# TensorE's expert program as a loop over pairs of experts, with every weight chunk in a fixed slot of the ring

## The chip, the cores and the metric

One core of one Trainium2 chip. The metric is the device time of one launch in microseconds (us): 1264.06 us, the median of 3 runs (1262.40 to 1265.34). One more execution was taken by the hardware profiler; it took 1263.88 us, of which 1262.1 us are the span of the trace, and 1.8 us lie outside it.

## The reference

One decoder block on 256 tokens of width 1024, float32. Two groups of four heads with gated recurrences share an input and an output projection; cross-attention into 256 memory tokens follows; then a mixture of 32 experts of which each token uses 4; then a norm. The experts are what matters here:

```
logits = h2 @ w_router + b_router ; top_v, top_i = top_k(logits, 4) ; gates = softmax(top_v)
for every expert e, on the tokens that chose it:
    gu = x @ w_gate_up[e] + b_gate_up[e]          # w_gate_up[e]: 1024 x 2048
    gate, up = min(gu[:, :1024], 7), clip(gu[:, 1024:], -7, 7)
    y += g * (((up + 1) * gate * sigmoid(1.702 * gate)) @ w_down[e] + b_down[e])   # w_down[e]: 1024 x 1024
```

The weights of one expert are 12.6 MB in float32, those of all 32 are 403 MB, and every one of them is read.

## The kernel before

The program is written out by hand for five engines, which meet only at semaphores. For the first 335 us TensorE does projections, recurrence, attention and router; then it does the experts one after the other.

An expert's weights come as six chunks of 2 MB (128 partitions x 4096 float32): chunks 0 to 3 are gate and up, 4 and 5 are down. Below, chunk e.k is chunk k of expert e, and its number is 6e+k. The chunks go through a ring of 11 places (`places`, `RING`), of which six double as the earlier panels' buffers and five as working buffers of the earlier stages. Chunk n has place n modulo 11. Chunks 0 to 10 are loaded by SyncE (SP) as their places come free in the earlier stages. From then on SP runs the loop

```
for n in range(RING, LOADS):
    before, k = (n - RING) // CHUNKS, (n - RING) % CHUNKS
    ...
    sp.wait_ge(sem["chunk_used"], sp.snap(used + (k + 1)))
    load_chunk(n)
```

so that chunk n is asked for once chunk n-11 has been used. SP works strictly in order: one load that waits holds all that come behind it. `chunk_used` is raised by TensorE after the last matmul on a chunk. How many chunks TensorE will have used by the end of an expert depends on the routing (an expert with more than 64 tokens is run again on the next 64), so SP reads that number from a table in memory. In this run every expert takes one block of 64.

TensorE's work for one expert (`pe.Fori(0, blocks)`): biases; 16 matmuls for each of chunks 0 to 3 (`pair`, L730, on the columns 0-63 and 64-127 of the array); `scatter` of the expert before (L740); a transpose of gates (L797); `gather` of the next expert's tokens (48 bf16 matmuls, L754, which pick the input features f of a tile with a stride through `h2_parts`); four transposes of the activations (L805); then 16 matmuls for each of chunks 4 and 5. All 32 experts are written out, each with its own places and its own counts as constants. VectorE and ScalarE follow in loops of their own.

Of the kernel before, what the change touches and what calls it, by code (L numbers as in the profile page):

```python
# [41 lines left out]
P = 128  # L42
D = 1024
T = 256
NT = T // P
KT = D // P
# [10 lines left out]
E = 32  # L57
# [3 lines left out]
ROWS = 64  # L61
MAXB = T // ROWS
# [3 lines left out]
GU_ROWS = KT // GU_CHUNKS  # L66
DOWN_ROWS = KT // DOWN_CHUNKS
LOADS = CHUNKS * E
RING = 11
MAXW = MAXB * E  # L70
WARM_UP = 14
BIAS_PARTS = (0, 2 * E, 3 * E)
PW = 512
# [39 lines left out]
def build(nc, A, out):  # L113

    ctx = ExitStack()
    with ctx:
        ctx.enter_context(nc.allow_non_contiguous_dma("small vectors are laid out by feature"))

        def sb(name, cols, dt=F32, rows=P):
            return ctx.enter_context(nc.sbuf_tensor(name, [rows, cols], dt))  # L120
# [12 lines left out]
        ring = sb("ring", SLOTS * 4096)  # L133
        slot6, slot7, slot8, slot9, slot10 = (sb(f"slot{k}", 4096) for k in range(6, 11))
        region5, region6 = slot6[:, 0:2048], slot6[:, 2048:4096]
        region1, region2 = slot7[:, 0:2048], slot7[:, 2048:4096]
        x_res_t, region10 = slot8[:, 0:2048], slot8[:, 2048:4096]
        s_t, row_t = slot9[:, 0:3072], slot9[:, 3072:4096]
        region3, tmp_t, late = slot10[:, 0:2048], slot10[:, 2048:3072], slot10[:, 3072:4096]
# [14 lines left out]
        def tm(t, off=0, n=D):  # L154

            return t[:, off:off + NT * n].rearrange("p (t n) -> p t n", n=n)
# [88 lines left out]
        def panel(n):  # L245

            s = n % SLOTS
            return ring[:, s * 4096:(s + 1) * 4096].rearrange("p (k n) -> p k n", n=PW)
# [3 lines left out]
        out_tile = tm(slot9, 0)  # L252
# [28 lines left out]
        def _(sp):  # L281
# [22 lines left out]
            def load_chunk(n):  # L304

                e, k = n // CHUNKS, n % CHUNKS
                dst, arrived = places[n % RING], chunk_in[n % RING]
# [5 lines left out]
                rows = DOWN_ROWS * P  # L313
                src = A["w_down"][0, e, (k - GU_CHUNKS) * rows:(k - GU_CHUNKS + 1) * rows, :].rearrange("(p a) n -> p (a n)", a=DOWN_ROWS)
                if n < LOADS - 1:
                    sp.dma_start(dst, src).then_inc(arrived, 16)
                    return
                half = DOWN_ROWS * D // 2
                sp.dma_start(dst[:, 0:half], src[:, 0:half]).then_inc(arrived, 16)
                sp.dma_start(dst[:, half:2 * half], src[:, half:2 * half]).then_inc(last_half_in, 16)  # L320

            wait_full(sp, "out11")
            load_chunk(0)
            wait_full(sp, "xq1")
            load_chunk(1)
            wait_full(sp, "xq3")
            load_chunk(2)
            wait_full(sp, "xv11")
            load_chunk(3)

            wait_full(sp, "pv3")
            load_chunk(4)
            load_chunk(5)
            wait_full(sp, "xo01")
            load_chunk(6)
            wait_full(sp, "xo11")
            load_chunk(7)

            load_chunk(8)
# [3 lines left out]
            load_chunk(9)  # L343
# [4 lines left out]
            load_chunk(10)  # L348
# [95 lines left out]
        def _(pe):  # L444
# [300 lines left out]
            def gather(ready):  # L745

                pe.wait_ge(sem["sel_ready"], ready)
                for c in range(GU_CHUNKS):
                    for a in range(GU_ROWS):
                        k = c * GU_ROWS + a  # L750
                        first = c * GU_ROWS * P + a
                        for i in range(3):
                            for t in range(NT):
                                last = pe.matmul(bank_a[:, k * ROWS:(k + 1) * ROWS],  # L754
                                                 h2_parts[:, i, t, first:first + GU_ROWS * P - a:GU_ROWS], sel[:, t, :],
                                                 start=(i == 0 and t == 0), stop=(i == 2 and t == NT - 1), skip_group_check=True)
                last.then_inc(sem["xb_psum"], 1)

            def chunk_of(e, k):

                n = e * CHUNKS + k
                return places[n % RING], chunk_in[n % RING], 16 * (n // RING + 1)
# [6 lines left out]
            for e in range(E):  # L769
                blocks = pe.value_load(table[0:1, e:e + 1], min_val=1, max_val=MAXB)  # L770
                first = pe.value_load(table[0:1, e + E:e + E + 1], min_val=0, max_val=MAXW)
                with pe.Fori(0, blocks) as c:
# [7 lines left out]
                    for k in range(GU_CHUNKS):  # L780
                        wk, arrived_k, count = chunk_of(e, k)
                        pe.wait_ge(arrived_k, count)
                        for a in range(GU_ROWS):
                            f = k * GU_ROWS + a
# [19 lines left out]
                    for a in range(DOWN_ROWS):  # L804
                        last = pe.matmul(bank_u[:, a * P:(a + 1) * P], act_t[:, a::DOWN_ROWS], ident[:, :], start=True,  # L805
                                         stop=True, is_transpose=True, skip_group_check=True)
# [4 lines left out]
                    for j in range(DOWN_CHUNKS):  # L811
                        wk, arrived_k, count = chunk_of(e, GU_CHUNKS + j)
                        pe.wait_ge(arrived_k, count)
                        for a in range(DOWN_ROWS):
                            if e == E - 1 and j == DOWN_CHUNKS - 1 and a == DOWN_ROWS // 2:
                                pe.wait_ge(last_half_in, 16)
                            f = DOWN_ROWS * j + a
                            last = pair(bank_d, actT[:, f, :], wk[:, a * D:(a + 1) * D], f == 0, f == KT - 1)
                        last.then_inc(sem["chunk_used"], 1)

# [619 lines left out]
```

## Time and profile before

| | |
|---|---|
| time, median of 3 runs | 1264.06 us |
| profiled execution / its span | 1263.88 us / 1262.1 us |
| TensorE matmuls busy (PE) | 1162.4 us, 92% |
| VectorE, ScalarE, GpSimd busy | 21%, 14%, 2% |
| read from HBM | 443.4 MB |
| loads of expert chunks | 46.4 to 47.9 us from issue to landing (medians) |
| the chain that ended last | PE 58%, DMA 38% |

PE's busy time is modelled at the ends of the matmuls, and in the experts' stage two matmuls run side by side in the array, so 92% does not say that TensorE is the bound. SPq is the queue of DMA issues that SP works through. "To landing" is the time from a DMA's issue to the last of its completions.

### The profile page before, as it was taken

The numbers are of one execution on the slowest core, as the hardware profiler recorded it, in microseconds if no ns is written. First come the engines' busy times: TensorE is split into PE (matmuls) and PEld (weight loads), VectorE is DVE, ScalarE is ACT, GpSimd is POOL, SyncE is SP. The second block draws the span as 40 slices with busy tenths as digits, with TensorE's granted clock in tenths as the row PEclk, the third lists the DMA queues.
The fourth block names the chain that finished last, engine by engine and source line by source line (L and its number), as shares of the span: only waits on it lengthen the run. The fifth ranks groups of instructions, "written<-read, shape, count | busy, mean of one in ns | idle before, by whom it ended". The sixth has DMA issues, their size and how long they took to land.

```text
span 1262.1 us, 16197 instructions
## 1 busy us (share of the span) xinstructions
PE 1162.4 (92%) x6670; PEld 567.8 (45%) x6670; DVE 268.7 (21%) x626; ACT 173.3 (14%) x284; POOL 28.0 (2%) x60
## 2 busy tenths in 40 slices
PE   8999999999799999999998888888888888888885
PEld 5955875875544444444443333333333333333332
DVE  4334455113612111121111111111111111111112
ACT  3222111023301110011100000010110010000001
POOL 3000010010200000000000000000000000000000
PEclk9999999999899999999999999999999999999999
DMA  8933300576799999999999999999999999999993
GB/s 262 365 133 133 133 10 1 210 257 241 274 419 426 429 427 427 428 427 428 426 428 427 428 428 426 428 427 427 428 428 427 427 427 427 427 429 427 427 427 138
DMA packets 53055, 445.42 MB, mean 353 GB/s; under 512 B 8896, under 2 KB 9312, under 8 KB 28192
## 3 DMA queue, kind: packets, MB, share of 16 engines
q1 hardware_dynamic: 52560, 442.87, 84.6%
q0 software_dynamic: 432, 1.59, 0.5%
q8 instruction: 54, 0.88, 0.3%
q14 instruction: 9, 0.07, 0.0%
HBM read 443.40 MB, written 1.05 MB: 352 GB/s over the span
## 4 chain that ended last, share of the span: by engine, by line
PE 58%; DMA 38%; issue 2%; DVE 2%; ACT 0%; SPq 0%; DVEq 0%
PE bank L730 26%; DMA ring<-in_w_gate_up 19%; DMA slot<-in_w_gate_up 19%; PE bank L504 12%; PE bank L495 7%; PE bank L740 3%; PE bank L754 3%; PE bank L515 2%; PE bank L474 1%; PE bank L805 1%; DMA ring<-in_w_in 1%; PE bank L797 1%; PE bank L617 1%; PE bank L668 1%; PE bank L649 1%
## 5 line engine op out<-in xcount | busy, mean ns | idle before, releaser
L730 PE MATMUL bank<-ring,region 128*64 128x512 f32 x1696 | 381.0, 596 | 41.7 <-DMA ring<-in_w_gate_up 28.3
L730 PE MATMUL bank<-slot,region 128*64 128x512 f32 x1376 | 309.9, 595 | 36.0 <-DMA slot<-in_w_gate_up 25.6
L730 PEld LDWEIGHTS bank<-ring,region 128*64 128x64 f32 x1696 | 133.7, 137 | 264.2 <-issue 207.2
L730 PEld LDWEIGHTS bank<-slot,region 128*64 128x64 f32 x1376 | 107.6, 137 | 218.2 <-issue 165.7
L1360 DVE TENSOR_SCALAR region<-bank 128x512 f32<-128x512 f32 x32 | 22.1, 691 | 713.3 <-PE bank L730 713.3
L504 PE MATMUL bank<-ring,slot 128*128 128x512 f32 x352 | 153.5, 594 | 0.1
L829 ACT ACTIVATE region<-bank 128x512 f32<-128x512 f32 (+2 forms) x136 | 72.8, 544 | 344.4 <-PE bank L730 231.2
L504 PEld LDWEIGHTS bank<-ring,slot 128*128 128x128 f32 x352 | 66.3, 190 | 79.9 <-issue 78.9
L829 ACT ACTIVATE bank<-region 128x512 f32<-128x512 f32 x32 | 19.3, 602 | 498.7 <-DVE region L1360 498.7
L495 PE MATMUL bank<-slot,ring 128*128 128x256 f32 x384 | 84.2, 380 | 0.0
L495 PEld LDWEIGHTS bank<-slot,ring 128*128 128x128 f32 x384 | 72.6, 190 | 10.4 <-issue 0.5
L740 PE MATMUL bank<-region 64*128 64x512 f32 x264 | 65.6, 615 | 0.7 <-ACT region L829 0.7
L754 PE MATMUL bank<-region,r_levels 128*128 128x64 bf16 x1584 | 52.8, 195 | 1.6 <-DVE region L1341 1.6
L754 PEld LDWEIGHTS bank<-region,r_levels 128*128 128x128 bf16 x1584 | 51.7, 99 | 2.2 <-issue 1.6
L740 PEld LDWEIGHTS bank<-region 64*128 64x128 f32 x264 | 22.7, 186 | 43.1 <-issue 41.5
L829 ACT ACTIVATE slot<-bank 128x512 f32<-128x512 f32 (+1 forms) x35 | 19.9, 586 | 100.7 <-PE bank L504 61.0
L1341 DVE TENSOR_SCALAR region<-region 128x64 bf16 (+1 forms) x64 | 13.3, 251 | 48.6 <-PE bank L754 45.8
L515 PEld LDWEIGHTS bank<-r_levels 128*128 128x128 f32 (+1 forms) x240 | 21.9, 189 | 3.6 <-issue 2.4
L1363 DVE TENSOR_SCALAR region<-bank 128x512 f32<-128x512 f32 x32 | 22.1, 691 | 5.3 <-PE bank L730 5.3
L805 PE MATMUL bank<-ident,region 128*128 128x128 f32 x128 | 23.2, 304 | 0.0
L515 PE MATMUL bank<-r_levels 128*128 128x128 f32 (+1 forms) x240 | 23.0, 281 | 0.0
L1367 DVE SCALAR_TENSOR_TENSOR region<-region 128x512 f32<-128x512 f32 x32 | 22.2, 692 | 3.3
(181 smaller groups left out, 493.8 us busy)
## 6 DMA issues: line engine op xcount, KB each, us to landing
ring<-in_w_gate_up SPq DMA_DIRECT2D x70, 2048.0 KB, 46.4
slot<-in_w_gate_up SPq DMA_DIRECT2D x58, 2048.0 KB, 47.9
ring<-in_w_down SPq DMA_DIRECT2D x36, 2048.0 KB, 47.8
slot<-in_w_down SPq DMA_DIRECT2D x27, 2048.0 KB, 47.6
ring<-in_w_in SPq DMA_DIRECT2D x7, 2048.0 KB, 19.4
ring<-in_w_xkv SPq DMA_DIRECT2D x4, 2048.0 KB, 8.0
ring<-in_w_out SPq DMA_DIRECT2D x2, 2048.0 KB, 7.6
ring<-in_w_xq SPq DMA_DIRECT2D x2, 2048.0 KB, 7.8
```

The costliest lines, as they stand in the source:

```text
L495: last = pe.matmul(bk[:, i * T:(i + 1) * T], w[:, k, (m + i) * P:(m + i + 1) * P], rhs[:, k, :], start=(k == 0), stop=(k == KT - 1))
L504: last = pe.matmul(bk[:, :], lhs[:, k, t * P:(t + 1) * P], w[:, k, :], start=(k == 0), stop=(k == KT - 1))
L515: return pe.matmul(out_, rows[:, j * P:(j + 1) * P], rows[:, i * P:(i + 1) * P], start=True, stop=True)
L730: last = pe.matmul(bk[half * ROWS:(half + 1) * ROWS, :], lhs, w[:, half * 512:(half + 1) * 512], start=start, stop=stop, skip_group_check= ...
L740: last = pe.matmul(bank_y[t][half][:, :], combT[rows, t * P:(t + 1) * P], yb[rows, :], start=False, stop=False, skip_group_check=True)
L754: last = pe.matmul(bank_a[:, k * ROWS:(k + 1) * ROWS], h2_parts[:, i, t, first:first + GU_ROWS * P - a:GU_ROWS], sel[:, t, :], start=(i == ...
L805: last = pe.matmul(bank_u[:, a * P:(a + 1) * P], act_t[:, a::DOWN_ROWS], ident[:, :], start=True, stop=True, is_transpose=True, skip_group ...
L829: return nc.scalar.activation(out_, in_, func, **kw)
L1341: ins = v.tensor_scalar(sel[:, t, :], rows, rank_m[:, t, e], None, ALU.is_equal)
L1360: v.tensor_scalar(g_t, bank_g[:, :], LIMIT, None, ALU.min).then_inc(sem["g_clamped"], 1)
L1363: v.tensor_scalar(u_t, bank_u[:, :], LIMIT, -LIMIT, ALU.min, ALU.max).then_inc(sem["u_clamped"], 1)
L1367: v.scalar_tensor_tensor(u_t, u_t, 1.0, g_t, ALU.add, ALU.mult).then_inc(sem["up_gated"], 1)
```

## The change

TensorE's 32 copies of an expert become 4 written-out experts (0 to 3, `HALVED`), a loop `pe.Fori(0, PAIRS)` of 13 passes with two experts in its body (4 to 29), and 2 written-out experts (30 and 31). A loop body needs the same addresses in every pass, so a chunk's place can no longer be n modulo 11. The new `slot_of` keeps the old places up to chunk 11 and then repeats every 12 chunks; a wait's count becomes a register that grows with the pass. The 11 slots are now one tensor, with the earlier buffers laid in so that chunks 0 to 10 lie over the same buffers as before.

```diff
-GU_ROWS = KT // GU_CHUNKS
+ROWS_PER = 4
+GU_TILES = KT // GU_CHUNKS
 RING = 11
+HALVED = 4
+PAIRS = (E - HALVED) // 2 - 1
...
-        places = [ring[:, s * 4096:(s + 1) * 4096] for s in (5, 1, 2, 0)] + [slot6[:, :], slot9[:, :]]
-        places += [ring[:, s * 4096:(s + 1) * 4096] for s in (3, 4)] + [slot7[:, :], slot8[:, :], slot10[:, :]]
+        def slot_of(e, k):
+
+            n = e * CHUNKS + k
+            if n <= RING:
+                return n % RING
+            if (e, k) == (E - 1, CHUNKS - 2):
+                return 0
+            j = n % (2 * CHUNKS)
+            return j + 1 if j < RING - 1 else j - 5
+
+        order = [(e, k) for e in range(E) for k in range(CHUNKS)]
+        loads_of = [[c for c in order if slot_of(*c) == s] for s in range(RING)]
+
+        def nth_load(e, k):
+            return loads_of[slot_of(e, k)].index((e, k)) + 1
+
+        def used_before(e, k):
+
+            return loads_of[slot_of(e, k)][nth_load(e, k) - 2]
...
-            def load_chunk(n):
+            def load_chunk(e, k):
...
-                    rows = GU_ROWS * P
-                    src = A["w_gate_up"][0, e, k * rows:(k + 1) * rows, :].rearrange("(p a) n -> p (a n)", a=GU_ROWS)
+                    rows, c0 = ROWS_PER * P, k % 2 * SLOT
+                    src = A["w_gate_up"][0, e, k // 2 * rows:(k // 2 + 1) * rows, :].rearrange("(p a) n -> p (a n)", a=ROWS_PER)
+                    sp.dma_start(dst, src[:, c0:c0 + SLOT]).then_inc(arrived, 16)
...
-            for n in range(RING, LOADS):
-                before, k = (n - RING) // CHUNKS, (n - RING) % CHUNKS
-                if k == 0 or n == RING:
-                    used = sp.value_load(table[0:1, before + 2 * E + 1:before + 2 * E + 2], min_val=0, max_val=CHUNKS * MAXW)
-                sp.wait_ge(sem["chunk_used"], sp.snap(used + (k + 1)))
-                load_chunk(n)
+            for e, k in order[RING:]:
+                before, kb = used_before(e, k)
+                used = sp.value_load(table[0:1, before + 2 * E + 1:before + 2 * E + 2], min_val=0, max_val=CHUNKS * MAXW)
+                sp.wait_ge(sem["chunk_used"], sp.snap(used + (kb + 1)))
+                load_chunk(e, k)
...
-                                                 h2_parts[:, i, t, first:first + GU_ROWS * P - a:GU_ROWS], sel[:, t, :],
+                                             h2_parts[:, i, t, c + a:c + ROWS_PER * P:ROWS_PER], sel[:, t, :],
...
-            for e in range(E):
+            for e in range(HALVED):
+                expert(e, slots(e), counts(e))
+            with pe.Fori(0, PAIRS) as i:
+                for odd in range(2):
+                    e = HALVED + odd
+                    per_pair = [n1 - n0 for n0, n1 in zip(counts(e), counts(e + 2))]
+                    n = {(m, n0): pe.snap(m * i + n0) for m, n0 in sorted(set(zip(per_pair, counts(e))))}
+                    expert(pe.snap(2 * i + e), slots(e), [n[m, n0] for m, n0 in zip(per_pair, counts(e))])
+            for e in range(E - 2, E):
+                expert(e, slots(e), counts(e), e == E - 1)
```

A gate-and-up chunk also holds other rows: before, partition p of chunk k had rows 2p and 2p+1 of 256 consecutive rows, so the chunk was 2 MB in one piece of memory. Now chunks 0 and 1 share 512 rows: partition p has rows 4p and 4p+1 of them in chunk 0 and 4p+2 and 4p+3 in chunk 1. A partition's piece is 16 KB as before, and the next partition's begins 32 KB on. The gather's stride through `h2_parts` goes from 2 to 4 elements with it.

TensorE's program shows the slots. First the two down chunks of expert 2, the biases of expert 3, and its chunks, in the program before (`chunk_in5` is the arrival semaphore of place 5; 64x512 is what one matmul writes):

```order
L730 MATMUL bank<-slot,region 64x512 [waits chunk_in5,actT_ready,comb_ready]
...
L730 MATMUL bank<-ring,region 64x512 [waits chunk_in6]
...
L730 MATMUL bank<-region 64x512 [waits one_hot_ready]
...
L730 MATMUL bank<-ring,region 64x512 [waits chunk_in7,xb_ready]
...
L730 MATMUL bank<-slot,region 64x512 [waits chunk_in8]
...
L730 MATMUL bank<-slot,region 64x512 [waits chunk_in9]
...
L730 MATMUL bank<-slot,region 64x512 [waits chunk_in10]
...
L730 MATMUL bank<-ring,region 64x512 [waits chunk_in0,actT_ready,comb_ready]
...
L730 MATMUL bank<-ring,region 64x512 [waits chunk_in1]
```

And the same place in the program after:

```order
L753 MATMUL bank<-ring,region 64x512 [waits chunk_in5,actT_ready,comb_ready]
...
L753 MATMUL bank<-ring,region 64x512 [waits chunk_in6]
...
L753 MATMUL bank<-region 64x512 [waits one_hot_ready]
...
L753 MATMUL bank<-ring,region 64x512 [waits chunk_in7,xb_ready]
...
L753 MATMUL bank<-ring,region 64x512 [waits chunk_in8]
...
L753 MATMUL bank<-ring,region 64x512 [waits chunk_in9]
...
L753 MATMUL bank<-ring,region 64x512 [waits chunk_in10]
...
L753 MATMUL bank<-ring,region 64x512 [waits chunk_in5,actT_ready,comb_ready]
...
L753 MATMUL bank<-ring,region 64x512 [waits chunk_in6]
```

Chunks 3.4 and 3.5 stood in slots 0 and 1; they now stand in slots 5 and 6, where chunks 2.4 and 2.5 are. Slot 0 is not used again until chunk 31.4. From expert 2 on the slots repeat: 1, 2, 3, 4, 5, 6 for an even expert and 7, 8, 9, 10, 5, 6 for an odd one.

SP's program is still written out, one load after the other. Before, from the load of chunk 20 to that of chunk 23:

```order
L311 DMA slot<-in_w_gate_up 128x4096 [waits chunk_used]
L354 REGISTER_ALU
L311 DMA slot<-in_w_gate_up 128x4096 [waits chunk_used]
L354 REGISTER_ALU
L316 DMA ring<-in_w_down 128x4096 [waits chunk_used]
L353 TENSOR_LOAD region
L353 ISA x2
L354 REGISTER_ALU
L316 DMA ring<-in_w_down 128x4096 [waits chunk_used]
```

After, from the load of chunk 20 to that of chunk 22:

```order
L335 DMA ring<-in_w_gate_up 128x4096 [waits chunk_used]
L376 TENSOR_LOAD region
L376 ISA x2
L377 REGISTER_ALU
L335 DMA ring<-in_w_gate_up 128x4096 [waits chunk_used]
L376 TENSOR_LOAD region
L376 ISA x2
L377 REGISTER_ALU
L340 DMA ring<-in_w_down 128x4096 [waits chunk_used]
```

The table is now read ahead of every load (L376), before only when the wait passed to another expert's chunks (L353). What the rows don't name is the count that is waited for: chunk 22 (3.4) waited for chunk 11 (1.5) and now waits for chunk 16 (2.4), chunk 23 for chunk 17 in place of 12, chunk 24 for chunk 12 in place of 13. From there on chunks 4 and 5 of an expert wait for chunks 4 and 5 of the expert before (6 back), and chunks 0 to 3 for those of two experts before (12 back).

The loop's end in TensorE's program after (L789 is the loop over blocks, L846 the loop over pairs):

```order
L753 MATMUL bank<-ring,region 64x512 [waits chunk_in6]
L753 MATMUL bank<-ring,region 64x512 x7
L789 REGISTER_ALU
L789 COMPARE_AND_BRANCH
L846 REGISTER_ALU
L846 COMPARE_AND_BRANCH
L787 TENSOR_LOAD region
```

The branch of L846 goes back over two experts, 12 times in a launch.

## Rows read from the trace of the kernel before

**Rows 1.** The page's 40 slices: PE busy, DMA engines busy, GB/s.
```profile
PE   8999999999799999999998888888888888888885
DMA  8933300576799999999999999999999999999993
GB/s 262 365 133 133 133 10 1 210 257 241 274 419 426 429 427 427 428 427 428 426 428 427 428 428 426 428 427 427 428 428 427 427 427 427 427 429 427 427 427 138
```
**Rows 2.** Chain that ended last, in order of time: start us, us, what.
```profile
340.50 15.28 PE bank L730 x68
...
413.22 21.25 PE bank L730 x100
...
439.46 21.25 PE bank L730 x100
...
465.69 21.25 PE bank L730 x100
...
936.62 3.65 PE bank L730 x16
...
945.25 3.67 PE bank L730 x16
...
995.32 3.65 PE bank L730 x16
...
1242.12 7.10 PE bank L730 x32
```
**Rows 3.** Windows: us, busy us (instructions) of five engines, PEclk, DMA share, GB/s.
```profile
353.00:401.00 48.00, 46.53 (x306) 20.80 (x304) 7.77 (x18) 5.48 (x10) 0.00 (x0) 1.00 1.01 428
401.00:417.00 16.00, 15.27 (x114) 7.09 (x112) 3.88 (x9) 2.15 (x4) 0.00 (x0) 1.00 1.00 427
660.00:1160.00 500.00, 442.08 (x2742) 175.28 (x2740) 66.06 (x153) 46.57 (x85) 0.00 (x0) 1.00 1.01 427
```
**Rows 4.** Single chunk loads of L311 and L316: form and issue time, then landing.
```profile
L316 SPq DMA_DIRECT2D ring<-in_w_down x1: 332/332/332, 345.5 to 345.5; - x1
DMA to landing us min/median/max: 7.7/7.7/7.7
...
L311 SPq DMA_DIRECT2D slot<-in_w_gate_up x1: 328/328/328, 390.7 to 390.7; - x1
DMA to landing us min/median/max: 12.8/12.8/12.8
...
L316 SPq DMA_DIRECT2D ring<-in_w_down x1: 328/328/328, 394.1 to 394.1; - x1
DMA to landing us min/median/max: 14.3/14.3/14.3
...
L311 SPq DMA_DIRECT2D slot<-in_w_gate_up x1: 327/327/327, 416.9 to 416.9; - x1
...
L311 SPq DMA_DIRECT2D ring<-in_w_gate_up x1: 328/328/328, 443.1 to 443.1; - x1
...
L311 SPq DMA_DIRECT2D ring<-in_w_gate_up x1: 1283/1283/1283, 1185.3 to 1185.3; - x1
DMA to landing us min/median/max: 47.9/47.9/47.9
```
**Rows 5.** SP's waits: who for whom, us in total, times, longest us.
```profile
SPq L311 <- PE bank L730: 382.7, 101, 9.3
```
**Rows 6.** Weight loads of 340 to 1250 us by form: busy us, mean ns.
```profile
L754 PEld LDWEIGHTS bank<-region,r_levels 128*128 128x128 bf16 x1536 | 49.1, 98 | 0.6 <-DVE stat L1407 0.3
L740 PEld LDWEIGHTS bank<-region 64*128 64x128 f32 x258 | 22.2, 186 | 42.6 <-issue 41.0 <-ACT region L829 1.6
L805 PEld LDWEIGHTS bank<-ident,region 128*128 128x128 f32 x128 | 17.9, 210 | 0.0
```
**Rows 7.** The page's DMA queues: packets, MB, share of 16 engines.
```profile
q8 instruction: 54, 0.88, 0.3%
```
**Rows 8.** The page's DMA issues: form, count, KB each, median us to landing.
```profile
ring<-in_w_xkv SPq DMA_DIRECT2D x4, 2048.0 KB, 8.0
```

More of the change, by code:

```diff
@@ L130, in build, with part @@
         banks = [ctx.enter_context(nc.psum_tensor(f"bank{b}", [P, 512], F32)) for b in range(8)]
[L133 to L139, printed above, removed]
+        ring = sb("ring", RING * SLOT)
+        def part(slot, first, last):
+            return ring[:, slot * SLOT + first:slot * SLOT + last]
+        panel_slots = (3, 1, 2, 6, 7, 0)
+        region5, region6 = part(4, 0, 2048), part(4, 2048, 4096)
+        s_t, row_t = part(5, 0, 3072), part(5, 3072, 4096)
+        region1, region2 = part(8, 0, 2048), part(8, 2048, 4096)
+        x_res_t, region10 = part(9, 0, 2048), part(9, 2048, 4096)
+        region3, tmp_t, late = part(10, 0, 2048), part(10, 2048, 3072), part(10, 3072, 4096)
         region7 = sb("region7", 3 * QT * T)
@@ L311, in load_chunk @@
                     sp.dma_start(dst, src).then_inc(arrived, 16)
                     return
[L313 to L318, printed above, removed]
+                half = SLOT // 2
                 sp.dma_start(dst[:, 0:half], src[:, 0:half]).then_inc(arrived, 16)
-                sp.dma_start(dst[:, half:2 * half], src[:, half:2 * half]).then_inc(last_half_in, 16)
+                sp.dma_start(dst[:, half:SLOT], src[:, half:SLOT]).then_inc(last_half_in, 16)
@@ L747, in gather @@
                 pe.wait_ge(sem["sel_ready"], ready)
[L748 to L754, printed above, removed]
-                                                 h2_parts[:, i, t, first:first + GU_ROWS * P - a:GU_ROWS], sel[:, t, :],
-                                                 start=(i == 0 and t == 0), stop=(i == 2 and t == NT - 1), skip_group_check=True)
+                for k in range(KT):
+                    c, a = k // ROWS_PER * ROWS_PER * P, k % ROWS_PER
+                    for i in range(3):
+                        for t in range(NT):
+                            last = pe.matmul(bank_a[:, k * ROWS:(k + 1) * ROWS],
+                                             h2_parts[:, i, t, c + a:c + ROWS_PER * P:ROWS_PER], sel[:, t, :],
+                                             start=(i == 0 and t == 0), stop=(i == 2 and t == NT - 1), skip_group_check=True)
                 last.then_inc(sem["xb_psum"], 1)
-            def chunk_of(e, k):
-                n = e * CHUNKS + k
-                return places[n % RING], chunk_in[n % RING], 16 * (n // RING + 1)
             gather(1)
@@ L767, in _, with expert @@
             pe.matmul(bank_d[0:1, MAXW:2 * MAXW], first_col, spans, start=True, stop=True).then_inc(sem["blocks_psum"], 1)
-            for e in range(E):
-                blocks = pe.value_load(table[0:1, e:e + 1], min_val=1, max_val=MAXB)
-                first = pe.value_load(table[0:1, e + E:e + E + 1], min_val=0, max_val=MAXW)
+            def expert(e, slots, counts, final=False):
+                blocks = pe.value_load(table[0:1, bass.ds(e, 1)], min_val=1, max_val=MAXB)
+                first = pe.value_load(table[0:1, bass.ds(e + E, 1)], min_val=0, max_val=MAXW)
                 with pe.Fori(0, blocks) as c:
@@ L780, in _ @@
                     for k in range(GU_CHUNKS):
[L781 to L784, printed above, removed]
+                        wk = part(slots[k], 0, SLOT)
+                        pe.wait_ge(chunk_in[slots[k]], counts[k])
+                        for a in range(GU_TILES):
+                            f = k * GU_TILES + a
                             last = pair(bank_g, xbT[:, f, :], wk[:, a * 2 * D:a * 2 * D + D], False, f == KT - 1)
@@ L803, in _ @@
                     pe.wait_ge(sem["act_ready"], w1)
-                    for a in range(DOWN_ROWS):
-                        last = pe.matmul(bank_u[:, a * P:(a + 1) * P], act_t[:, a::DOWN_ROWS], ident[:, :], start=True,
+                    for i in range(DOWN_ROWS):
+                        last = pe.matmul(bank_u[:, i * P:(i + 1) * P], act_t[:, i::DOWN_ROWS], ident[:, :], start=True,
                                          stop=True, is_transpose=True, skip_group_check=True)
```

49 lines of the change are left out of this document (28 added, 21 removed).

## The prediction
> **What bounds the kernel now.** I read the busy slices first. Counted from 0, a slice is 31.55 us. From slice 12 (about 379 us) to slice 38 the DMA engines are full (digit 9 throughout) at 425 to 429 GB/s, and PE's digit sinks from 9 to 8 halfway [rows 1]. So in the experts' stage the transfers are the bound at least in the second half. The windows say the same more closely: 428 GB/s at a DMA share of 1.01 from 353 to 401 us, 427 from 401 to 417, and 427 from 660 to 1160 us, where PE is busy 442 of 500 us [rows 3]. The reader should see that there is no free transfer time anywhere from 353 us to the end: whatever the DMA engines lose there, the end loses too, if nothing gives it back.
>
> Then the chain in order of time, for TensorE's pace. Early, the matmuls of chunks e.4 and e.5 and of the next expert's chunks 0 to 3 begin at 413.22, 439.46, 465.69 us: 26.23 us for one expert, with no wait for a load between them. Later they begin at 936.62 and 995.32 us with one expert between: 29.35 us for one [rows 2], which is six chunks at 4.89 us. So TensorE begins late (340.50 us), with eleven chunks in the ring or on the way; it needs 3.1 us less per expert than the DMA engines do, and it catches up with them around 650 us (PE's digit is 9 up to slice 20). Up to there TensorE does not set the end either; it only frees places, and the free places are what keeps the DMA engines busy.
>
> How much stock there is at that time is seen from single loads. A chunk asked for at 345.5 us, with the engines nearly idle, landed after 7.7 us. One asked for at 390.7 us took 12.8, at 394.1 us 14.3, at 1185.3 us 47.9 us [rows 4]. What is over 7.7 us is queueing behind other chunks. At 394.1 us, then, only 14.3 - 7.7 = 6.6 us of transfers stood ahead of the new one. That is the number on which the change turns: a load that comes more than 6.6 us later than this one does finds idle engines.
>
> **The change, part by part.**
>
> *The slots.* Up to chunk 21 every load waits for the same chunk as before. Chunk 22 (3.4) is the one asked for at 394.1 us: its place was free once chunk 11 (1.5) was used. It will now need slot 5, where chunk 16 (2.4) is. TensorE begins chunk 2.4 at 413.22 us [rows 2] and the load that waits for just that use today, chunk 27, is issued at 416.9 us [rows 4]. So chunk 22 is asked for at 416.9 instead of 394.1 us, 22.8 us later. The last load before it, chunk 21, lands at 390.7 + 12.8 = 403.5 us, so the engines stand idle from there until about 418 us. Chunk 22 finds them idle and lands at 416.9 + 7.7 = 424.6 us, where today it lands at 394.1 + 14.3 = 408.4 us. The loss is 16.2 us (22.8 less the 6.6 us of queue that are gone).
>
> Is TensorE held up by this? It needs chunk 22 at 439.5 us [rows 2], after it has landed; no. Does the stream stop again? Chunk 23 needs chunk 17 used, 3.4 us after chunk 16, and is queued by then. Chunks 24 to 27 need nothing new (12 back) and go out at once. They end at 424.6 + 5 x 4.89 = 449.1 us. Chunk 28 (4.4) waits for chunk 22, and the load that waits for that use today is issued at 443.1 us [rows 4]; a lone load needs 7.7 - 4.9 = 2.8 us before its data flow, so it is in time with 449.1 - 443.1 - 2.8 = 3.2 us to spare. From then on TensorE gains 3.1 us per expert on the transfers and the spare grows, until TensorE waits for loads again. In that state chunk e.4's matmuls end 945.25 + 3.67 - 936.62 = 12.3 us after those of chunk e.3 could begin [rows 2], that is after its arrival, while 6 x 4.89 = 29.4 us of transfers were queued at that arrival (down to chunk 3 of the next expert): 29.4 - 12.3 - 2.8 = 14 us to spare at every wait. So one dry spell and no second.
>
> Does anything give the 16.2 us back? In the steady stretch the stream is full and the chain ends with the last chunks and 7.10 us of matmuls at 1242.12 us [rows 2]; the work behind it is untouched. No. The cover that hid a short ring before was the queue of 6.6 us, and it is used up.
>
> *Source of the chunks.* 28 x 4 = 112 gate-and-up chunks behind the dry spell are now read in 16 KB pieces at a stride of 32 KB. The pieces are as long as before on both sides. The trace has no such load; the nearest row is the panel of w_xkv in short rows, 8.0 us to landing [rows 8] against 7.7 for a lone chunk, 0.3 us more each, so up to 112 x 0.3 = 34 us, and as much below nothing if a spread source should be read faster. I take 0: 16 KB pieces are nearest to the chunks themselves.
>
> *Gather.* The weights of its 48 matmuls are read at a stride of 8 bytes, not 4. In the trace, float32 weights at 16 bytes stride (L805) take 210 ns and contiguous ones (L740) 186 ns; L754 takes 98 ns at 4 bytes [rows 6]. So the bound is 24 ns each, 1.15 us a gather, and four of them lie ahead of the use of chunk 16: 0 to 4.6 us on top of the dry spell; a gain has no reason. I take 0, since most of a weight load runs beside the matmuls. The Trainium skill ("SBUF — State Buffer", Door 1: The DMA port swizzle, the note on cachelines) says that reads go at full rate as long as two fall in one 16-byte line, which bf16 at a stride of 4 just does; by it this term is 0, and no row here shows a bf16 load at that stride.
>
> *SP's table reads.* One register load ahead of every chunk load. SP waited for TensorE 101 times for 382.7 us ahead of gate-and-up loads alone [rows 5], 3.8 us each, and the reads stand ahead of the waits: they vanish in that time. In the dry spell too, since SP sits in chunk 22's wait from about 391 us. 0; if the cover were gone, under 1 us once.
>
> *Loop, branches, register counts.* TensorE's own pace would give an end of its matmuls at 340.5 + 32 x 26.23 = 1179.9 us; they end at 1249.2 us [rows 2], 16.2 us later after the change. So the loop's 12 ways back can cost 85.5 / 12 = 7.1 us each before the end feels them. A way back may have to fetch the program again. The row for fetches shows 54 pages, 0.3% of 16 engines' span [rows 7]: 0.003 x 16 x 1262.1 / 54 = 1.1 us a page. The whole program before, with 32 copies, is 54 pages in 16 KB units, so a body of two experts is about 3 pages: 3.4 us one behind the other. I take 0 at the end. If fewer pages are fetched, their transfer time comes back, and for that the stream itself gives a bound: chunk 22 landed at 408.4 us and chunk 189 at 1185.3 + 47.9 = 1233.2 us, 4.94 us a chunk against 4.89 undisturbed. All of that difference, 167 x 0.047 = 7.8 us, is the most there is to gain.
>
> **Sum**, against the profiled execution: 1263.88 + 16.2 + 0 + 0 + 0 = 1280.1 us. The median is 0.2 us above that execution, so 1280 us is also the number for the median. Ends of the small terms: -7.8 (stream undisturbed) and +4.6 (gather), with 4 us for a spell that is somewhat longer because of the 3.2 us of spare at chunk 28: 1272 to 1289 us.
>
> **The rivals.**
>
> *The loop stalls TensorE past its cover.* For it: nothing in this trace has a body of that length, and the price per page is worked out from a rounded share. Against: 7.1 us per way back are a lot beside 3.4. If a way back cost 10 us, the end would go 12 x 2.9 = 35 us further, 1315 us. The Trainium skill ("Runtime: NRT & Kernel Launch", Instruction fetch mechanics) speaks against the change here: it says that a taken branch to a page outside the current two stalls for the fetch, and that kernels therefore prefer unrolled code. By the page alone there would be a stall at each of the 12 ways back; it gives no duration, and by the rows it stays within the cover.
>
> *The strided source is slower.* At the bound of rows 8, 34 us more: 1314 us. Against: equal pieces.
>
> *No dry spell.* The change would not do what its slots say, or the engines would have more in their queue at 403 us than the landing times show: 1264 us. Against: 14.3 us to landing leaves no room for 22.8 us.
>
> *Not slower, by a faster stream.* Place: the 112 gate-and-up chunks from 3.4 on. Price: to win back 16.2 us each must take 0.145 us less than 4.89, 3%; from there it decides the sign. At 4% the time is 1280.1 - 22 = 1258 us. For it: the pieces of one chunk now lie wider apart in memory. Against: no slice shows more than 429 GB/s [rows 1], with gate-and-up and down chunks alike, which looks like the engines' own limit.
>
> **How the numbers follow.** The forecast (one dry spell) 0.80, with 1272 to 1289 us for itself; loop stall 0.05; slower source 0.06; no dry spell 0.05; faster stream 0.04, half of it below 1261.5 us. A measurement of this kernel tells 0.2%, 2.5 us, from no change. Faster: 0.02. Same: 0.05 from no dry spell and 0.02 from the faster stream, 0.07. Slower: 0.91. The range 1271 to 1291 us is the forecast's own with a little for smaller shares of the last two terms; all other cases lie outside and hold no more than 0.2.
>
> **What the profile after would show.** The DMA digits of slices 12 and 13 (379 to 442 us) fall to about 7 and GB/s to some 330 there, alone. Chunk 22's load is issued near 417 us and takes 7.7 us to landing. All later landings are 16 us late. TensorE begins to wait for loads at about 530 instead of 650 us (chunk 4.3 lands at 449 us and is wanted at 457, and 8 us are gone in 2.6 experts at 3.1 us each). A down chunk of the steady stretch, asked for 12.3 us after chunk 3 of the expert before arrived, lands seven chunks after that one: 7 x 4.89 - 12.3 = 22 us from issue to landing, with no loss of GB/s. PE's way back shows a gap of a few us at most, every 58.7 us. I am wrong if the digits stay 9 around 410 us, if slices behind 442 us fall below 425 GB/s, or if the trace shows PE's waits, not the loads', ahead of the last experts.

## The result and the profile after

| | before | after |
|---|---|---|
| median of 4 runs | 1263.23 us | 1275.57 us |
| ratio, 95% interval | | 1.0102 (1.0081 to 1.0123) |
| profiled execution / span | 1263.88 / 1262.1 us | 1275.52 / 1273.8 us |

The change makes the kernel slower by 12.3 us in the medians and 11.7 us in the spans. The forecast was 1280 us with a range of 1271 to 1291.

The page's slices after (PE, DMA engines, GB/s; they answer to [rows 1], and a slice is 31.8 us) and its instruction queue, which answers to [rows 7]:

```profile
PE   8999999999899999988888888888888888888885
...
DMA  8933300766795999999999999999999999999993
GB/s 267 355 132 132 132 10 1 269 234 248 280 430 231 386 426 428 428 428 429 429 428 428 429 428 430 428 428 428 429 428 428 428 429 428 428 428 429 429 428 158
...
q8 instruction: 22, 0.36, 0.1%
```

One hole, in slice 12 (382 to 414 us) and the start of 13, and full engines from there to the end, at 428 to 430 GB/s behind slice 14 where before it was 425 to 429. PE's digit falls to 8 at slice 17 instead of 21: TensorE catches up with the transfers sooner.

SP's issues around the hole (start us, duration, what):

```profile
389.16 0.33 SPq L335 DMA_DIRECT2D ring<-in_w_gate_up  x1
415.58 3.76 SPq L340 DMA_DIRECT2D ring<-in_w_down  x2
420.00 3.29 SPq L335 DMA_DIRECT2D ring<-in_w_gate_up  x4
```

and single loads with their times to landing, which answer to [rows 4] (chunks 21, 22, 28 and 189):

```profile
L335 SPq DMA_DIRECT2D ring<-in_w_gate_up x1: 328/328/328, 389.2 to 389.2; - x1
DMA to landing us min/median/max: 12.3/12.3/12.3
...
L340 SPq DMA_DIRECT2D ring<-in_w_down x1: 327/327/327, 415.6 to 415.6; - x1
DMA to landing us min/median/max: 7.6/7.6/7.6
...
L340 SPq DMA_DIRECT2D ring<-in_w_down x1: 328/328/328, 442.0 to 442.0; - x1
DMA to landing us min/median/max: 11.9/11.9/11.9
...
L335 SPq DMA_DIRECT2D ring<-in_w_gate_up x1: 328/328/328, 1206.0 to 1206.0; - x1
DMA to landing us min/median/max: 38.6/38.6/38.6
```

Chunk 21 is in at 401.5 us, chunk 22 is asked for at 415.6 and is in 7.6 us later. A window in between says the rest (columns as in [rows 3]):

```profile
402.00:415.00 13.00, 12.27 (x101) 5.97 (x98) 3.89 (x9) 2.14 (x4) 0.00 (x0) 1.00 0.01 1
```

TensorE is at full work (12.27 of 13 us) while the DMA engines stand at 1%. TensorE waits for nothing there, and still this is where the time goes.

The landings of three chunks divide the 11.7 us (times in us):

| | before | after | difference |
|---|---|---|---|
| chunk 11 lands | 353.2 | 351.3 | -1.9 |
| chunk 11 to chunk 22 | 55.2 | 71.9 | +16.7 |
| chunk 22 to chunk 189 | 824.8 | 821.4 | -3.4 |
| chunk 189 to the end of the span | 28.9 | 29.2 | +0.3 |

So there are three things to explain: a dry spell of 16.7 us, a stream that is 3.4 us faster behind it, and 1.9 us ahead of the experts.

### The profile page after: what moved, and what is told of

Read it like the earlier page. It is cut to its first block, busy times and chain, and to the rows that moved or that the text cites. A ratio compares the mean times of both kernels' runs of the same rounds, so it can differ in the third digit from the quotient of the medians.

```text
span 1273.8 us, 16753 instructions
## 1 busy us (share of the span) xinstructions
PE 1164.6 (91%) x6670; PEld 554.2 (44%) x6671; DVE 269.1 (21%) x626; ACT 173.2 (14%) x284; POOL 28.0 (2%) x60
## 4 chain that ended last, share of the span: by engine, by line
PE 52%; DMA 40%; SPq 3%; DVE 2%; issue 2%; ACT 1%; DVEq 0%
DMA ring<-in_w_gate_up 39%; PE bank L753 21%; PE bank L527 12%; PE bank L518 7%; PE bank L763 3%; PE bank L775 3%; SPq L376 2%; PE bank L538 2%; PE bank L497 1%; ACT region L863 1%; SPq L335 1%; PE bank L691 1%; PE bank L672 1%; PE bank L814 1%; PE bank L640 0%
## 5 line engine op out<-in xcount | busy, mean ns | idle before, releaser
L753 PE MATMUL bank<-ring,region 128*64 128x512 f32 x3072 | 683.5, 595 | 87.9 <-DMA ring<-in_w_gate_up 60.6
L753 PEld LDWEIGHTS bank<-ring,region 128*64 128x64 f32 x3072 | 223.6, 137 | 507.6 <-issue 384.5
L527 PE MATMUL bank<-ring 128*128 128x512 f32 x352 | 153.4, 593 | 0.0
L527 PEld LDWEIGHTS bank<-ring 128*128 128x128 f32 x352 | 66.2, 190 | 79.6 <-issue 78.9
L518 PE MATMUL bank<-ring 128*128 128x256 f32 x384 | 84.1, 380 | 0.0
L518 PEld LDWEIGHTS bank<-ring 128*128 128x128 f32 x384 | 72.6, 190 | 10.5 <-issue 0.5
L775 PE MATMUL bank<-region,r_levels 128*128 128x64 bf16 x1584 | 59.0, 199 | 1.6 <-DVE region L1375 1.5
L775 PEld LDWEIGHTS bank<-region,r_levels 128*128 128x128 bf16 x1584 | 58.6, 118 | 1.9 <-issue 1.6
L863 ACT ACTIVATE ring<-bank 128x512 f32<-128x512 f32 (+1 forms) x35 | 19.9, 586 | 98.8 <-PE bank L527 59.1
L1375 DVE TENSOR_SCALAR region<-region 128x64 bf16 (+1 forms) x64 | 13.4, 252 | 48.6 <-PE bank L775 45.8
L1405 DVE TENSOR_TENSOR region<-region,bank 128x512 f32<-128x512 f32 x32 | 22.0, 687 | 1.1
L863 ACT ACTIVATE r_levels<-ring 128x1024 f32<-128x1024 f32 (+1 forms) x14 | 14.6, 1053 | 53.6 <-DVE ring L1269 34.0
## 6 DMA issues: line engine op xcount, KB each, us to landing
ring<-in_w_gate_up SPq DMA_DIRECT2D x128, 2048.0 KB, 30.8
ring<-in_w_down SPq DMA_DIRECT2D x63, 2048.0 KB, 21.6
```

The lines of the kernel that those rows point to most:

```text
L518: last = pe.matmul(bk[:, i * T:(i + 1) * T], w[:, k, (m + i) * P:(m + i + 1) * P], rhs[:, k, :], start=(k == 0), stop=(k == KT - 1))
L527: last = pe.matmul(bk[:, :], lhs[:, k, t * P:(t + 1) * P], w[:, k, :], start=(k == 0), stop=(k == KT - 1))
L753: last = pe.matmul(bk[half * ROWS:(half + 1) * ROWS, :], lhs, w[:, half * 512:(half + 1) * 512], start=start, stop=stop, skip_group_check= ...
L775: last = pe.matmul(bank_a[:, k * ROWS:(k + 1) * ROWS], h2_parts[:, i, t, c + a:c + ROWS_PER * P:ROWS_PER], sel[:, t, :], start=(i == 0 and ...
L863: return nc.scalar.activation(out_, in_, func, **kw)
```

## The experiments

Theory 1, worked out after the result: the one jump of a wait (chunk 22 from 11 back to 6 back) makes the dry spell, and the loop makes the stream faster, because fewer pages of instructions are fetched beside it. Rivals: the smaller ring costs all along; the new rows of a chunk, or the shorter queue of loads, change the stream. In the results, "stream" is the time from the landing of chunk 22 to that of chunk 189, and ratios are to the kernel before, run on the same chip.

**Unrolled again (unrolled).** Fixed slots and all else of the change, no loop:

```diff
-            for e in range(HALVED):
-                expert(e, slots(e), counts(e))
-            with pe.Fori(0, PAIRS) as i:
-                ...
-            for e in range(E - 2, E):
+            for e in range(E):
                 expert(e, slots(e), counts(e), e == E - 1)
```

> The changed kernel with its fixed slots, its chunk rows and its gather, but TensorE's 32 experts written out again. Theory 1: the 3.4 us that the stream won back behind the dry spell (chunk 22 to chunk 189 took 821.4 us, before 824.8) come from the instruction pages that the loop saves (22 instead of 54 on q8). Then pages go back to about 54, the dry spell stays (chunk 22 asked for 26 us after chunk 21), and the time is about 3 us over the changed kernel's, some 16 us over before. Rival: the 3.4 us come from the shorter queue of loads or from the new rows of the chunks; then this kernel takes the changed kernel's time, 12 us over before, whatever q8 shows.

Measured: 1280.95 us, ratio 1.0145 (1.0129 to 1.0160); 54 pages; stream 825.0 us. Its page:

```profile
GB/s 269 350 132 132 132 10 1 252 244 244 285 428 233 384 428 427 429 426 429 426 428 427 428 427 428 428 425 429 427 428 427 427 427 428 427 427 428 427 426 152
...
q8 instruction: 54, 0.88, 0.3%
```

The same hole (233 and 384), and behind it before's rate again. Without the loop the median is 5.4 us higher, where 3 had been expected, and 18 us over before. In the two profiles 3.6 us of this lie in the stream; 1.8 us lie ahead of chunk 11's landing (353.1 against 351.3 us), where no loop has begun yet (the last point of the next section).

**The idle slot put to use (slot0).**

```diff
-            if (e, k) == (E - 1, CHUNKS - 2):
-                return 0
...
-            return j + 1 if j < RING - 1 else j - 5
+            return j + 1 if j < RING - 1 else (5, 0)[j - RING + 1]
```

> The changed kernel, with the eleventh slot (0), which it leaves idle, given to chunk 5 of every odd expert; chunk 5 then waits 12 chunks back, chunk 4 still 6 back. Theory 1: what costs time is the one jump of chunk 22's wait from chunk 11 to chunk 16, which stays, so the time is the changed kernel's within 1 us, 12 us over before. Rival: the smaller ring itself (10 slots in use, 2 of them twice) costs time all along; then this one is clearly faster than the changed kernel, by several us.

Measured: 1275.68 us, ratio 1.0106 (1.0091 to 1.0122), the changed kernel's time; stream 821.0 us. An eleventh slot in use gives nothing: with ten slots the steady stretch lost nothing.

**Only the rows (rows_only).** Before, with the new source of the chunks and the gather's stride:

```diff
-                    rows = GU_ROWS * P
-                    src = A["w_gate_up"][0, e, k * rows:(k + 1) * rows, :].rearrange("(p a) n -> p (a n)", a=GU_ROWS)
-                    sp.dma_start(dst, src).then_inc(arrived, 16)
+                    rows, c0 = ROWS_PER * P, k % 2 * 4096
+                    src = A["w_gate_up"][0, e, k // 2 * rows:(k // 2 + 1) * rows, :].rearrange("(p a) n -> p (a n)", a=ROWS_PER)
+                    sp.dma_start(dst, src[:, c0:c0 + 4096]).then_inc(arrived, 16)
```

> The kernel before, unrolled and with its ring of 11, and only the new rows of a gate-and-up chunk (16 KB pieces at a stride of 32 KB) and the gather's stride of 4. Theory 1: the source costs nothing and the gather 0.2 us per expert on TensorE, which is not the bound: 0 us, within 1 us of before. Rival: the new source makes the stream faster and is what gave 3.4 us back: 1260 us, 3 us under before. If it made it slower, some of the loss of the change were its work.

Measured: 1263.97 us, ratio 1.0008 (0.9999 to 1.0017); stream 825.0 us. The strided source costs the stream nothing. The rival that the new rows gave the 3.4 us falls.

**The fixed slots begin at expert 13 (late13).** Chunk n keeps slot n modulo 11 up to expert 12; from 13 on the fixed slots, numbered so that they join on; the loop runs over experts 15 to 30. The same edit with 5, 7 and 9 for `FIXED`, and another slot for chunk 31.4, makes three more kernels below.

```diff
-            if n <= RING:
+            if n < FIXED * CHUNKS:
                 return n % RING
...
-            j = n % (2 * CHUNKS)
-            return j + 1 if j < RING - 1 else j - 5
+            j = (n - FIXED * CHUNKS) % (2 * CHUNKS)
+            return (FIXED * CHUNKS + (j if j < RING - 1 else j - CHUNKS)) % RING
```

> The changed kernel, with the old ring (chunk n in slot n modulo 11) kept up to expert 12 and the fixed slots from expert 13 on; the loop then runs over experts 15 to 30 (8 passes). At expert 14 a load asked for 22.8 us later still finds over 24 us of queue ahead of it. Theory 1: no dry spell, DMA digits of 9 throughout, and the saved instruction pages (about 14 fewer) stay as a gain: 0 to 2 us under before, about 1262 us. Rival (the short ring or the loop itself costs): still 5 to 12 us over before.

Measured: 1258.97 us (11 runs), ratio 0.9970 (0.9961 to 0.9979). No hole, and the rate of the looped kernel:

```profile
DMA  8933300665799999999999999999999999999994
GB/s 274 356 134 134 134 10 1 224 258 230 277 422 428 427 427 427 429 425 430 426 425 431 426 426 430 427 427 428 430 427 428 429 428 428 429 429 428 428 429 166
...
q8 instruction: 35, 0.57, 0.2%
```

It beats both kernels, by 3 us more than expected. The loop and the short ring do no harm here; the moment at which the short ring begins does.

**From expert 5 (late5).**

> The changed kernel with the old ring up to expert 4 and the fixed slots from expert 5 on; the loop runs over experts 7 to 30 (12 passes). The load that jumps from 11 to 6 back is now that of chunk 40 (6.4), asked for at 472.8 us before, 24.1 us from issue to landing less 7.7, so 16.4 us of queue ahead of it. Theory 1: its dry spell is 22.8 - 16.4 = 6.4 us, in place of 16.7 (10.3 us less than in the changed kernel): about 1265.5 us, with the idle stretch near 495 us instead of 410. Rival (something else of the slots or the loop costs, whenever they begin): 1272 us or more.

Measured: 1267.59 us, ratio 1.0035 (1.0023 to 1.0046). The hole has moved to slice 15 and is smaller:

```profile
DMA  8933300666799997999999999999999999999993
GB/s 251 374 135 133 133 10 1 238 253 232 283 429 427 427 429 307 430 428 429 427 428 429 427 428 429 428 427 429 429 426 429 429 427 428 430 426 428 431 428 155
```

and the load that jumps, chunk 40, finds idle engines:

```profile
L341 SPq DMA_DIRECT2D ring<-in_w_down x1: 327/327/327, 495.0 to 495.0; - x1
DMA to landing us min/median/max: 7.6/7.6/7.6
```

From chunk 11's landing to chunk 40's it takes 150.8 us, before 143.4: a spell of 7.4 us against 6.4 expected. TensorE's experts take a little longer here (below), so the load is asked for 23.9 us later than before, counted from chunk 11's request. In the trace of before chunk 40 takes 23.8 us to landing, so 16.1 us stood ahead of it (the expectation has 24.1 and 16.4); 23.9 - 16.1 = 7.8. The median is 2 us over the one expected.

**From expert 7 (late7).**

> The same with the fixed slots from expert 7 on, the loop over experts 9 to 30 (11 passes). Chunk 52 (8.4) has 22 us of queue ahead of it and comes 22.8 us later. Theory 1: a dry spell of 0 to 2 us, and the loop's gain on the stream as in late13: 1259 to 1261 us. Rival (the gain of late13 came from its few passes): slower than late13 by 3 us or more.

Measured: 1260.47 us, ratio 0.9981 (0.9970 to 0.9993). Chunk 52 lands 203.9 us after chunk 11, before 203.5: a spell of 0.4 us. In the trace of before it takes 31.4 us to landing, so the queue ahead of it was 23.7 us and not 22, and it is now asked for 24.3 us later: 0.6 us by the same subtraction. Its stream took 822.5 us, 2 us more than in the two kernels that begin later: the landing shows the engine that is last, and those ahead of it, with less in their queues, stood idle for some 3.6 us (end of this section).

**Only two passes in the loop (loop2).** Fixed slots as in the change, `HALVED = 26`:

> The changed kernel, same slots, but with experts 4 to 25 written out too, so that only the last two of the 13 passes are in a loop (26 to 29). It saves hardly any instruction pages: about 50 instead of 22 on q8. Theory 1 (the stream is faster because pages are no longer fetched beside it): 1279 to 1281 us, like the unrolled kernel, 167 chunks in about 825 us. Rival (what helps is something that the loop's code does once, such as its register waits, or the size of the program as it is loaded): nearer to the changed kernel's 1275.6 us.

Measured: 1280.45 us, ratio 1.0130 (1.0112 to 1.0148), 51 pages, stream 824.5 us: the unrolled kernel's time. That the program has a loop in it gains nothing; how much of it is looped does.

**Late slots without a loop (late13_unrolled).** `FIXED = 13`, all experts written out:

> Old ring up to expert 12, fixed slots from 13 on, no loop at all. Theory 1: no dry spell and no saved pages, so the time of before within 1 us (1263 us), and late13's 4 us under before are all the loop's. Rival (the shorter queue of loads, 6 back, is what makes the stream faster): 1259 us as late13. The clock's dip to half speed near 182 us, which the three kernels without a loop showed and the three with one did not, would show here again if it hangs on the loop.

Measured: 1263.94 us, ratio 1.0002 (0.9993 to 1.0011), 54 pages, stream 824.9 us. The shorter queue of loads does nothing for the stream; late13's gain is the loop's.

**Seven passes (loop7).** `HALVED = 16`:

> The changed kernel, same slots, with experts 4 to 15 written out and the last 7 passes (experts 16 to 29) in the loop: about 37 instruction pages on q8, between the 22 of the changed kernel and the 51 of loop2. Theory 1 (each page fetched beside the stream delays one of the 16 transfer engines, and a chunk lands with the slowest): 167 chunks in 821 to 823 us, 1276 to 1278 us. If late13 was no accident, where 35 pages cost nothing, it is at 821 us. Rival (not the pages, but the loop's code in the rest of the program): nearer to 825 us, 1280 us.

Measured: 1278.21 us, ratio 1.0112 (1.0098 to 1.0127), 38 pages, stream 821.7 us. The median is 0.2 us above the upper end of what was expected, the stream in the lower half of its range. By the stream, the 16 pages more than in the changed kernel cost 0.3 us, and the 13 further ones of loop2 cost 2.8. So the gain does not go in proportion to the pages; what it goes with is seen at the end of this section.

**From expert 9 (late9).**

> Old ring up to expert 8, fixed slots from 9 on, loop over experts 11 to 30 (10 passes): the earliest start at which theory 1 sees no dry spell (the queue ahead of chunk 64 is over 24 us), with a few pages fewer than late13. A candidate for the fastest: 1257.5 to 1259.5 us. Rival (the gain hangs on something else than the spell and the pages): over 1261 us.

Measured: 1260.01 us (6 runs), ratio 0.9968 (0.9956 to 0.9981), stream 820.4 us, no hole. The time is 0.5 us above what was expected; the ratio is late13's.

**More pages, same loop (late13_pages).** late13, with code on idle GpSimd that does nothing:

```diff
+            for _ in range(8000):
+                pool.wait_ge(sem["rest_ready"], 1)
```

> late13 with 8000 waits on a semaphore that has long been reached, on GpSimd, which is idle in the experts' stage: they do nothing, but their code has to be fetched, about 31 pages more, beside the stream. Theory 1 (fetched pages slow the stream): the 4 us of late13 under before are lost, 167 chunks in 824 us or more, 1262 to 1264 us. Rival (pages cost nothing, the loop gains in another way): 1259 us as late13.

Measured: 1275.19 us, ratio 1.0097 (1.0083 to 1.0112), 16 us over late13 and some four times what was expected. In the two profiles the spans differ by 16.1 us: 1.3 us lie ahead of chunk 11's request, where hardly any of the added code has been fetched (this profile has the dip of TensorE's clock that is told of below, late13's has not), 0.8 in its landing, 0.9 from there to that of chunk 22, and 13.2 in the stream. The waits were merged in pairs (4000 of them ran), and their pages came on the other instruction queue, 43 packets where late13 has 12:

```profile
q14 instruction: 43, 0.35, 0.1%
```

How can 0.25 MB hold up the transfers by 15 us? Windows from 342 to 684 us, where the added pages fall, first of this kernel, then of late13:

```profile
342.00:684.00 342.00, 320.09 (x1990) 137.93 (x1986) 47.05 (x110) 32.91 (x60) 0.00 (x0) 1.00 1.01 426
```

```profile
342.00:684.00 342.00, 332.46 (x2102) 148.29 (x2100) 50.98 (x119) 35.65 (x65) 0.00 (x0) 1.00 1.00 425
```

The engines' mean share and the bytes are the same. But a chunk asked for in that stretch (chunk 60) lands 12 us later; late13_pages first, then late13:

```profile
L336 SPq DMA_DIRECT2D ring<-in_w_gate_up x1: 328/328/328, 559.6 to 559.6; - x1
DMA to landing us min/median/max: 47.6/47.6/47.6
```

```profile
L336 SPq DMA_DIRECT2D ring<-in_w_gate_up x1: 328/328/328, 558.3 to 558.3; - x1
DMA to landing us min/median/max: 35.6/35.6/35.6
```

A chunk has landed when its last part has. The trace file holds 16 completions for every load, which I read as one for each DMA engine. Of chunk 60 in late13_pages fifteen come within 4 us, and the last one 11.8 us behind them; in late13 all sixteen lie within 3.6 us. For chunk 76 the last one comes 16.5 us behind the other fifteen. So one engine falls behind, and the others run ahead into later chunks. From chunk 22 to chunk 60 the landings lose 10.3 us for some 20 pages. Later the ring shortens, the engines that are ahead run out of loads (392 GB/s and a share of 0.94 in this window), and the lag becomes lost transfer:

```profile
700.00:740.00 40.00, 35.55 (x210) 13.84 (x208) 3.89 (x9) 3.33 (x6) 0.00 (x0) 1.00 0.94 392
```

Which engine fetched the pages is not in the trace. Nor does a run carry out the 4000 waits from a loop, without fetching their code, so it is not shown by itself that the fetching and not the waits does it; that one DMA engine alone falls behind while they are fetched speaks for the fetching.

All streams without added pages together: 824.5 to 825.0 us in the five kernels with 51 to 54 pages on q8, 820.4 to 822.5 in the six with 22 to 38, and 829.4 - 7.4 = 822.0 in late5, whose spell lies inside. The completions tell where the difference arises. From the first completion of chunk 22 to the first of chunk 189 it is 817.0 to 817.5 us in all ten kernels without added pages and without a spell behind chunk 22, loop or no loop (820.8 in late7 and 826.7 in late5, which have one). What differs is how far the last completion of a chunk lies behind its first. From chunk 22 to chunk 189 this distance grows from 1.9 to 9.7 us before, from 0.9 to 8.5 in unrolled, 1.0 to 8.2 in loop2, 1.0 to 5.2 in loop7 and 0.8 to 4.8 in the changed kernel. So the foremost engine is never slower; with more of the program in the loop the hindmost one falls back less, and in loop7, with 16 pages more than the changed kernel, hardly more than there. How the pages fall on the engines is not in the trace.

## Why the prediction was right, step by step

**The dry spell: right, in place and size.** 16.2 us were forecast, 16.7 measured. Counted from the request of chunk 11, that of chunk 22 came at 415.6 - 343.6 = 72.0 us, before at 394.1 - 345.5 = 48.6: 23.4 us later, 22.8 forecast, the queue ahead had been 6.6 us, and the landing took 7.6 us as a lone load's does. What is over comes from the gather (next but one). The unrolled kernel shows the same spell without the loop (425.1 - 353.1 = 72.0 us from chunk 11 to 22), and moving the start of the fixed slots to experts 5, 7, 9 and 13 takes it to 7.4, 0.4, 0 and 0 us: the rule "lateness of the request less the queue ahead of it" gives 16.8, 7.8 and 0.6 us for starts at experts 2, 5 and 7, and holds over the range tried.

**No second spell: right.** Chunk 28 was asked for at 442.0 and took 11.9 us, 4.2 us of them in the queue, where 3.2 us had been left to spare. The down chunks' median is 21.6 us to landing (22 forecast) with no loss of rate; that of the gate-and-up chunks 30.8:

```profile
ring<-in_w_gate_up SPq DMA_DIRECT2D x128, 2048.0 KB, 30.8
ring<-in_w_down SPq DMA_DIRECT2D x63, 2048.0 KB, 21.6
```

Nothing gave the spell back. TensorE waited for loads from about 537 us (530 forecast).

**The source of the chunks: right, 0** (rows_only).

**The gather: too low, and inside its bound.** Its weight loads take 117 ns, before 98 [rows 6]:

```profile
L775 PEld LDWEIGHTS bank<-region,r_levels 128*128 128x128 bf16 x1488 | 54.3, 117 | 0.0
```

rows_only, with the new stride and neither slots nor loop, has 118. 19 ns each is close to the 24 ns of the bound, by luck in part: L740 loads 64 partitions and L805 128, so their difference was not the price of a stride alone. Only 0.2 us of each 48 reach TensorE's pace (1.60 instead of 1.40 us a gather in the chain). Three gathers ahead of chunk 16's use make 0.6 us. By the note on cachelines of the Trainium skill's page "SBUF — State Buffer" a stride of 4 bf16 should have been free; here the trace does not agree.

**The loop on TensorE: right that it does not reach the end, wrong in the mechanism.** I reckoned with about 3 pages fetched at each of 12 ways back. There were none: 22 pages in the whole launch, fewer than 12 x 3, and between 495 and 1225 us the trace has no packet on q8. And the matmuls run through each of the 12 ways back with no idle time ahead of the next expert's biases. The first one (bf16 are the biases):

```profile
491.50 7.09 PE L753 MATMUL bank<-ring,region 128*64 128x512 f32 x32 [0.88 <-ACT region L863]
498.42 0.61 PE L753 MATMUL bank<-region 128*64 128x512 bf16 x4
498.85 1.46 PE L753 MATMUL bank<-ring,region 128*64 128x512 f32 x6
```

The body of two experts stayed on the chip. The page "Runtime: NRT & Kernel Launch" of the Trainium skill (Instruction fetch mechanics) says that a taken branch to a page outside the current two waits for a fetch, which with a body of about 3 pages would be each of these; the measurement decides otherwise. An expert takes 26.6 us in the loop, before 26.23 [rows 2], of which 0.2 are the gather:

```profile
438.33 21.25 PE bank L753 x100
...
464.93 21.25 PE bank L753 x100
...
491.50 7.11 PE bank L753 x32
```

**The saved pages: mis-sized.** The forecast of 1280.0 is 4.4 us above the median; the larger part is this term. It stood in the sum as 0, with up to 7.8 us as its end, because I took the body to be fetched again in every pass. Measured: 3.4 us of stream in the profiles (3.6 against the unrolled kernel). The bound was sound: 817.0 to 817.5 us by the first completions is what 167 chunks at 4.89 us make. The medians with and without the loop differ by 5.4 us, but 1.8 us of that lie ahead of the experts in the profiles. By the table of landings the forecast was 4.5 us too high: 3.4 from here and 1.9 from ahead of the experts, less 0.5 at the spell and 0.3 at the end.

**The slices: wrong in detail.** I forecast two digits of 7 and some 330 GB/s; it was 5 and 231, then 9 and 386. The spell came 2 us earlier and the slices of a longer span are wider, so most of it fell in one slice.

**The 1.9 us ahead of the experts: not forecast.** TensorE's granted clock was 0.50 (1.2 GHz) for 3.4 us in the profile of before, right behind 24 matmuls of one or two columns (179.0 to 181.8 us), and 1.00 in that of after, behind the same 24 matmuls. Before, then after, then the kernel from expert 7, which has a loop and shows the dip too:

```profile
182.20:185.40 3.20, 3.20 (x17) 3.20 (x17) 1.26 (x5) 0.00 (x0) 2.91 (x6) 0.50 0.20 45
```

```profile
182.20:185.40 3.20, 3.20 (x31) 3.20 (x30) 2.76 (x9) 0.00 (x0) 2.91 (x7) 1.00 0.24 46
```

```profile
182.20:185.00 2.80, 2.80 (x15) 2.80 (x14) 0.74 (x3) 0.18 (x1) 2.46 (x5) 0.50 0.22 54
```

The matmuls behind it (48 of them) take 7.23 us with the dip and 5.60 without, 1.6 us. Of the 13 profiles nine show it and four don't: all four kernels without a loop do, and five of the nine with one. So a loop alone does not remove it; whether it comes by chance stays open. Two profiles alone therefore can't settle a difference of 2 us between kernels.

## What to carry to other kernels

When a ring of buffers feeds a saturated stream, ask of every slot reuse how much later the request comes and how much is queued ahead of it at that moment; the difference was lost for good here, where the stream was full to the end, though TensorE did not wait. A shorter ring was free once the queue was deep, so a layout that a loop needs should begin where the stock has built up: here from expert 9 or 13 the loop is 0.3% faster than the unrolled kernel, from expert 2 it is 1% slower. In a kernel bound by all DMA engines together, straight-line code is traffic too, and what counts is how far it sets back the hindmost engine.

## What the runs showed of the hardware

- A loop body of two experts of TensorE's program was run 13 times with 22 pages fetched in the launch and no idle time of TensorE at any of the 12 ways back.
- With 0.25 MB more on an instruction queue, from 4000 waits on GpSimd, the loads landed 15 us later (late13_pages less late13, counted from chunk 11's request); the waits themselves were not tried without their pages. 32 pages less gained 3.4 to 3.6 us of stream.
- Time from issue to landing can grow by 12 us at the same mean share and GB/s of the DMA engines: the last of the 16 completions came 11.8 us behind the other fifteen, so landing shows the slowest engine, the page's digits the mean.
- The foremost of the 16 completions kept its pace in all ten kernels without added pages or a later spell (817.0 to 817.5 us for 167 chunks); only the last one fell further behind it, by 3.2 to 4.2 us in the five kernels with 22 to 38 pages and by 7.2 to 7.9 in the five with 51 to 54.
- Reading 16 KB pieces at a stride of 32 KB instead of one block of 2 MB cost nothing (825.0 against 824.8 us for 167 chunks).
